# Second mixer of a two-block network: the two attention heads of a pair in common steps, kept cumulative sums, and scan products ordered by kind

## The reference

```python
# 8 heads of 64: strictly causal stick-breaking attention
z = q @ k.T * 64 ** -0.5
log_keep = where(valid, -softplus(z), 0)
log_rest = cumsum(log_keep, reverse=True) - log_keep
attn = where(valid, exp(log_sigmoid(z) + log_rest), 0);  o = attn @ v
# 8 heads of 64: RWKV-7 recurrence, one token after the other
sa = S @ (-kk_t)
S = S * w_t + outer(sa, kk_t * a_t) + outer(v_t, k_t);   y_t = S @ r_t
```

## Time and profile before

| | us |
|---|---|
| three runs: median (lowest, highest) | 2177.69 (2170.0, 2178.99) |
| the profiled execution, its time | 2169.75 |
| its span | 2168.5 |
| TensorE busy | 1991.5 (92%) |
| VectorE, ScalarE, GpSimd busy | 794.9, 705.6, 763.2 |
| chain that ended last: TensorE's share of the span | 28% (L489, the products with weights: 19%) |

### The profile page before, as it was taken

The page is one execution under the profiler, slowest core; times in us unless marked ns, Lnnn a source line. Parts: engine busy times, 40 slices in busy tenths (PEclk is TensorE's granted clock), DMA queues, the critical chain, the costliest instruction groups (busy, mean ns, idle before and its releaser), DMA issues. The chain is left out here.

```text
span 2168.5 us, 32158 instructions
## 1 busy us (share of the span) xinstructions
PE 1991.5 (92%) x13960; PEld 1674.6 (77%) x13960; DVE 794.9 (37%) x1065; ACT 705.6 (33%) x1056; POOL 763.2 (35%) x444
## 2 busy tenths in 40 slices
PE   3889988999999999999999888888999789999997
PEld 2657767777888889999999877866666568888885
DVE  6664453232111013443310466643443433434201
ACT  2453221333222333222222333254554333222222
POOL 2322120434444554444444332211111144444453
PEclk9999999999999999999999999998998899999999
DMA  7332220324332232232222422100000322332331
GB/s 272 115 119 98 79 79 32 116 78 145 117 97 90 90 102 88 88 94 91 84 88 93 131 59 63 30 6 2 2 2 2 126 69 89 96 97 89 98 91 62
DMA packets 55723, 182.76 MB, mean 84 GB/s; under 512 B 7552, under 2 KB 7808, under 8 KB 55456
## 3 DMA queue, kind: packets, MB, share of 16 engines
q1 hardware_dynamic: 55584, 180.72, 25.4%
HBM read 175.45 MB, written 5.24 MB: 83 GB/s over the span
## 5 line engine op out<-in xcount | busy, mean ns | idle before, releaser
L2090 POOL TENSOR_TENSOR WL<-RAWS,WH 128x1024 fp32r<-128x1024 f32 (+2 forms) x275 | 649.0, 2363 | 983.4 <-ACT WH L1622 983.4
L489 PE MATMUL PS<-HH,WH 128*128 128x264 f32 (+2 forms) x2184 | 673.1, 350 | 48.4 <-issue 12.9
L489 PE MATMUL PS<-HL,WH 128*128 128x264 f32 (+2 forms) x2184 | 657.4, 343 | 0.0
L489 PE MATMUL PS<-HH,WL 128*128 128x264 f32 (+2 forms) x2184 | 654.3, 341 | 0.0
L489 PEld LDWEIGHTS PS<-HH,WH 128*128 128x128 f32 (+1 forms) x2184 | 380.7, 192 | 117.4 <-issue 36.6
L1622 ACT ACTIVATE WH<-RAWS 128x1024 fp32r<-128x1024 f32 (+2 forms) x275 | 283.9, 1033 | 455.1 <-PE PS L489 402.1
L489 PEld LDWEIGHTS PS<-HH,WL 128*128 128x128 f32 (+1 forms) x2184 | 380.5, 191 | 48.4 <-issue 0.4
L489 PEld LDWEIGHTS PS<-HL,WH 128*128 128x128 f32 (+1 forms) x2184 | 380.9, 191 | 47.1 <-issue 1.6
L489 PE MATMUL PS<-IHf,WH 128*128 128x512 f32 (+1 forms) x704 | 209.4, 338 | 0.0
L489 PE MATMUL PS<-IHf,WL 128*128 128x512 f32 (+1 forms) x704 | 209.2, 338 | 0.0
L489 PE MATMUL PS<-ILf,WH 128*128 128x512 f32 (+1 forms) x704 | 209.2, 338 | 0.0
(11 more groups left out here) (493 smaller groups left out, 1917.0 us busy)
## 6 DMA issues: line engine op xcount, KB each, us to landing
RAWS<-w_w_in SPq DMA_DIRECT2D x52, 512.0 KB, 4.3
RAWS<-w_ada SPq DMA_DIRECT2D x32, 512.0 KB, 3.6
RAWS<-w_f0g SPq DMA_DIRECT2D x22, 512.0 KB, 3.6
RAWS<-w_f0u SPq DMA_DIRECT2D x22, 512.0 KB, 3.5
RAWS<-w_f1g SPq DMA_DIRECT2D x22, 512.0 KB, 3.6
RAWS<-w_f1u SPq DMA_DIRECT2D x22, 512.0 KB, 3.6
RAWS<-w_f2g SPq DMA_DIRECT2D x22, 512.0 KB, 3.5
RAWS<-w_f2u SPq DMA_DIRECT2D x22, 512.0 KB, 3.5
```

The costliest lines, as they stand in the source:

```text
L489: ins = te.matmul(ps[0:m, q, o:o + b - a] if len(halves) > 1 else ps[0:m, o:o + b - a], w[:, k * m:k * m + m], v[:, k0 + k, a:b], start=fi ...
L2090: ge.tensor_tensor(WL[s % NS][:, 0:n], RAW[i % NR][:, 0:n], WH[s % NS][:, 0:n].bitcast(f32), ALU.subtract).then_inc(*w_lo.up(s))
```

## The change

- `heads(b)` becomes `heads()`: both heads of a pair take each stage one after the other, in ten ticks a step instead of five. The round becomes five ticks of the recurrence and four of the heads. ATT_TICKS goes from 107 to 50.
- The sum of the masked values of all blocks done so far is kept: GpSimd adds the previous tile to the present one, ScalarE and VectorE split the sum into high and low parts at column 512 of KHI and KLO, and one pair of all-ones products takes the place of one per earlier block. Blocks' own parts all lie at column 0 (the first one at 512, where it is its own sum).
- The scan's value products read SV's lower half directly with 64 rows; V0, its zeros and its copy go, and `after_copy` with them.
- The scan's products with the state all come before those with the values, in both groups.
- `gn_g` and `gn_hi` become one semaphore each, in the same order.

```diff
-ATT_TICKS = 107
+ATT_TICKS = 50
@@ tensor, rw_scan
-            te.wait_ge(*rv0.at(n))
+            te.wait_ge(*ra[e].at("v", t))
...
             for i in range(4):
                 for par, q in enumerate(HALF):
-                    te.matmul(PS[q, 6, 64 * i:64 * i + 64], AR[:, i, n, 0, :], SB[:, i, par, :], start=True, stop=False)
-                    ins = te.matmul(PS[q, 6, 64 * i:64 * i + 64], MM[e][:, 2 * i + par, 0:64], V0[:, 2 * i + par, :],
-                                    start=False, stop=True)
+                    te.matmul(PS[q, 6, 64 * i:64 * i + 64], AR[:, i, n, 0, :], SB[:, i, par, :], start=i == 0, stop=False,
+                              skip_group_check=True)
+            for i in range(4):
+                for par, q in enumerate(HALF):
+                    ins = te.matmul(PS[q, 6, 64 * i:64 * i + 64], MM[e][64:128, 2 * i + par, 0:64],
+                                    SV[e][64:128, 2 * i + par, :], start=False, stop=True, skip_group_check=True)
...
                 for i in range(4):
                     te.matmul(PS[:, 6, 64 * i:64 * i + 64], SB[:, i, :, :].rearrange("p a t -> p (a t)"),
-                              AR[:, i, n, 1, :], start=True, stop=True)
-                    for par in range(2):
...
+                              AR[:, i, n, 1, :], start=i == 0, stop=False, skip_group_check=True)
+                for h in range(8):
+                    i, par = divmod(h, 2)
+                    ins = te.matmul(PS[64 * par:64 * par + 64, 6, 64 * i:64 * i + 64], SV[e][:, h, :],
+                                    MM[e][:, h, 64:128], start=False, stop=True, skip_group_check=True)
@@ tensor, heads
+                    for b, q in enumerate(HALF):
+                        te.matmul(PS[:, b, 0:n], KA[q, i, 128 * j:128 * j + 128], QA[q, i, 512 - n:512], start=True,
+                                  stop=True).then_inc(*hp[b].up("z", r))
+                    for _ in range(7):
+                        yield
+                    for b in range(2):
+                        te.wait_ge(*hd[b].at("lo", r))
                         for part in (KHI[b], KLO[b]):
+                            ins = te.matmul(PS[:, b, 0:n], TRIR[:, :], part[:, KAT[x]:KAT[x] + n], start=False, stop=True,
+                                            skip_group_check=True)
+                        if x:
+                            if x > 1:
+                                te.wait_ge(*hl.at(6 * i + 2 * x - 4 + b))
+                            m = LEN[j + 1]
+                            for part in (KHI[b], KLO[b]):
+                                ins = te.matmul(PS[:, b, n - m:n], ONER[:, :], part[:, 512:512 + m], start=False,
+                                                stop=True, skip_group_check=True)
+                        ins.then_inc(*hp[b].up("c", r))
+                    for _ in range(3):
+                        yield
...
                 for j in range(5):
+                    for b, q in enumerate(HALF):
+                        h = 2 * i + b
+                        ins = te.matmul(PS[q, b, 512 - LEN[j]:512], VT[:, j, 64 * h:64 * h + 64],
+                                        ATT[b][:, OFF[j]:OFF[j] + LEN[j]], start=(j == 0), stop=(j == 4))
@@ on every engine; vector and scalar with attention_parts() behind
-        alternate(rk, heads(0), rk, later_by(2, heads(1)))
+        rk, both = pipeline(NCH, rw_prepare, rw_scan), heads()
+        alternate(rk, both, rk, both, rk, both, rk, both, rk)
@@ vector: max-add at tick 4, then at tick 5 (x > 1) this, lower part at tick 6
+        def lower_sum(i, x, b):
+            n = LEN[BLOCKS[x]]
+            ve.wait_ge(*hh.at(6 * i + 2 * x - 2 + b))
+            ve.scalar_tensor_tensor(KLO[b][:, 512:512 + n], TT[b][(5 * i + x) % 2][:, 0:n], -1.0,
+                                    KHI[b][:, 512:512 + n].bitcast(f32), ALU.mult,
+                                    ALU.subtract).then_inc(*hl.up(6 * i + 2 * x - 2 + b))
@@ scalar: Abs, Exp, Ln of both heads at ticks 0, 1, 2, at 3 (x > 1) this, upper parts at 5, Exp into ATT at 8
+        def upper_sum(i, x):
+            r, n = 5 * i + x, LEN[BLOCKS[x]]
+            for b in range(2):
+                ae.wait_ge(*ht.at(6 * i + 2 * x - 2 + b))
+                ae.activation(KHI[b][:, 512:512 + n], TT[b][r % 2][:, 0:n], ACT.Copy,
+                              scale=-1.0).then_inc(*hh.up(6 * i + 2 * x - 2 + b))
@@ gpsimd: masks at ticks 4 and 9, between them at tick 7
+                    if x in (1, 2, 3):
+                        for b in range(2):
+                            t = TT[b][r % 2][:, 128:n]
+                            ge.wait_ge(*hd[b].at("lo", r))
+                            if x > 1:
+                                ge.wait_ge(*ht.at(6 * i + 2 * x - 4 + b))
+                            ge.tensor_tensor(t, t, TT[b][(r - 1) % 2][:, 0:n - 128],
+                                             ALU.add).then_inc(*ht.up(6 * i + 2 * x - 2 + b))
```

More of the change, by code:

```diff
@@ L933, in heads @@
                     r, n = 5 * i + x, LEN[j]
[L934 to L942, removed]
@@ L1529, in rw_scan, with heads @@
             yield
-        def heads(b):
+        def heads():
             for i in range(4):
@@ new lines, in heads @@
+                    for b in range(2):
+                        t = TT[b][r % 2]
+                        ve.wait_ge(*ha[b].at("ln", r))
+                        ve.scalar_tensor_tensor(t[:, 0:n], PS[:, b, 0:n], 0.0, t[:, 0:n], ALU.max,
+                                                ALU.add).then_inc(*hd[b].up("m", r))
+                        if j == 0:
+                            ve.wait_ge(*hd[b].at("m", r))
+                            ve.wait_ge(*fz.at("pm"))
+                            ve.tensor_scalar(t[:, 0:n], t[:, 0:n], PM[:, 0:1], None, ALU.mult).then_inc(*hm[b].up(i))
@@ L1561, in attention_parts @@
                                  ALU.subtract).then_inc(*cat2_lo.up(j))
-        ve.wait_ge(*rz.at("v0"))
-        ve.wait_ge(*rz.at("sb"))
+        ve.wait_ge(*rz.at(0))
         for s in s_bs:
             ve.wait_ge(s, 16)
-        rk = pipeline(NCH, rw_prepare, rw_scan)
-        alternate(rk, heads(0), rk, later_by(2, heads(1)), attention_parts())
+        rk, both = pipeline(NCH, rw_prepare, rw_scan), heads()
+        alternate(rk, both, rk, both, rk, both, rk, both, rk, attention_parts())
         def group_norm(i):
@@ L1992, in rw_scan, with heads @@
             yield
-        def heads(b):
-            pb, a = 64 * b, ha[b]
+        def heads():
             for i in range(4):
@@ L2007, in heads @@
-                    ae.activation(t, t, ACT.Ln, bias=1.0).then_inc(*a.up("ln", r))
+                    t = [TT[b][r % 2][:, 0:n] for b in range(2)]
+                    for b in range(2):
+                        ae.wait_ge(*hp[b].at("z", r))
+                        if x >= 2:
+                            ae.wait_ge(*ht.at(6 * i + 2 * x - 4 + b))
+                        ae.activation(t[b], PS[:, b, 0:n], ACT.Abs).then_inc(*ha[b].up("abs", r))
+                    yield
+                    for b in range(2):
+                        ae.wait_ge(*ha[b].at("abs", r))
+                        ae.activation(t[b], t[b], ACT.Exp, scale=-1.0).then_inc(*ha[b].up("exp", r))
```

151 lines of the change are left out of this document (66 added, 85 removed).

## The result

The change takes the kernel from 2176.26 us (median of 4 runs, 2170.0 to 2178.99) to 2155.66 us (4 runs, 2154.93 to 2156.39): a ratio of 0.991, with a 95% interval of 0.9893 to 0.9926. The direction was right, about a third of the size came.

What follows compares the result with a forecast made beforehand. It took the chain of a block, not TensorE's 220 us, as the new bound: four pairs of 60.6 us, 242, plus 3 make a 245 us mixer, 52 us less, so 2118, forecast 2120 us, range 2090 to 2155.

Steps and rivals of the forecast that it cites:

- What TensorE would save: Second mixer: 47 us less TensorE work, from 266.9 us busy to 220.
- The output pair: Two heads' products with the values, alternating column halves, overlap: about 3.2 us instead of 2 x 3.11, 12 us in all.
- The score pair: Two heads' score products on different row halves overlap: 1.5 us at 512 columns against 2 x 1.06, 10 us in all.
- The scan's output products: Ordered by kind in each of 8 scans: 1.3 us instead of 2.52, 9.8 us in all.
- Rival 3: The pairs of heads' products don't overlap on TensorE's array, 22 us come back: about 2135 us, chance 0.06.
- the loss of up to 12 us: By the Trainium skill's rule on weight loads, little of the output pair's 12 us would come.
- The static order: Five recurrent to four pair ticks a round: recurrence and attention end together, removing the last chunk's 40 us tail.
- The chain of a block: Dependent stages from scores to next scores as the mixer's new bound: 60.6 us a pair, 13.6 at x = 4.
- Rival 2: Queues in step bind each other, 1.5 us more in each of 20 blocks: mixer 275 us, time 2150, chance 0.17.
- Other engines: In the mixer ScalarE about 149 us busy, VectorE 140, GpSimd 51 of some 240; none becomes the bound.
- After the mixer: Output-weight and bonus loads and VectorE's wait for the bonus stay; cost 0, or 2.5 us without that cover.
- rival 4: TensorE's clock held low in the mixer: at a share of 0.6, 330 us and time 2203; chance 0.05.

Runs made afterwards that it cites:

- e5: Changed kernel with the output products of one head before those of the other instead of alternating: 2165.23 us, ratio 0.995 against the kernel before.
- e4: Changed kernel with only the scan's output products back in the old order, value products following each product with the state: 2167.58 us, ratio 0.9966 against the kernel before.
- e7: Changed kernel with four recurrent ticks instead of five to four of the heads in each round: 2171.05 us, ratio 0.9972 against the kernel before.
- e3: Kernel before with one more recurrent tick in each round, nothing else of the change: 2178.36 us, ratio 1.0021 against the kernel before.
- e1: Changed kernel made serial in the mixer, on every engine all recurrence first, then all paired heads: 2259.25 us, ratio 1.0384 against the kernel before.
- e13: Changed kernel with the recurrence one tick later in VectorE's queue only: 2149.39 us, ratio 0.9884 against the kernel before.
- e8: Changed kernel without the kept sums, each earlier block having its all-ones products again: 2151.59 us, ratio 0.99 against the kernel before.

## Why the prediction was wrong, point by point

1. *What TensorE would save: right.* 47 us forecast, 54 measured, as busy time. 64 all-ones products are left (eight rows of eight in the groups by shape), as said. The output pair, 20 products, holds TensorE from 1557.77 to 1560.93: 3.16 us, forecast 3.2, against 3.11 for one head in the earlier trace rows. The score pair at 512 columns holds it from 1537.97 to 1539.03: 1.06 us, forecast 1.5; it takes as long as one head did in the earlier trace rows. The scan's output products take 1.65 us (1539.65 to 1541.30), forecast 1.3, before 2.52: 7 us in eight scans, forecast 9.8. Rival 3 is out, and so is the loss of up to 12 us that the prediction set against the output pair; e5 (+9.6) and e4 (+12) show that these edits reached the time of the kernel.
2. *The static order as a gain of its own: too large.* The prediction calls it "the largest single effect". The tail did go: the last state update is at 1690.7 and the heads end 10 us later, twice the 5 us said. But the forecast let the 40 us vanish at the price of 0.64 us a recurrent tick. e7 shows what the removal gives in the paired form, 19 us of mixer for 44 us of tail. e3, meant to test it on the kernel before, made a new tail and settles nothing.
3. *The chain of a block: the step that failed.* The sum of 60.6 us a pair measured 68.4, mostly in x = 4, 13.6 forecast and 19.4 measured. The stages themselves were right: the second lower part is done 8.5 us after the scores' start in e1 (third pair), and the forecast's 9.1 to 9.7 less its 1.1 us of recurrent work is 8.0 to 8.6. What was wrong stands between the stages. Each recurrent operation there was priced at its length, 0.25 to 0.6 us. It should have been priced at the time when its own input arrives. Of the 14.9 us of the block above, 3.5 are such a wait before the first Exp, and more follow on VectorE and TensorE. The cumulative products were priced at full clock, which is 6.6 us of the whole. So x = 4 costs 23 us more over four pairs, and x = 2, whose waits were not taken apart, 8: together the 29 us between 245 and 274, the other blocks being about level and the forecast having 3 us in reserve.
4. *The recurrence as a chain: missing.* It was counted as TensorE work, 159 us, that fills gaps. e1 shows that it is 172 us long by itself, 145 of them busy. Two chains of 172 and, at a low clock, 207 us in fixed queues had to be laid into each other within 245; the forecast had no term for that.
5. *Rival 2 is what happened.* It gave 275 us of mixer and 2150 at a chance of 0.17; measured are 274 and 2155.7. Its price was spread evenly, 1.5 us in each of 20 blocks; in fact two of the five block lengths carry it, so that its sum came out is in part luck. The sign that it named (TensorE waits for recurrent copies) and the forecast's (for the lower part) both came, because each chain holds the other. e1 is the evidence for that: with the recurrence out of the way, scores to cumulative products at x = 4 fall from 13.6 to 8.2 us on average. e13 shows that the two waits trade: an edit that only changes which of the two comes first on VectorE takes 11 us from the one and gives 4 to the other.
6. *Other engines: sizes near, sign of the trade missed.* VectorE 132.5 of 140 forecast, ScalarE 133.3 of 149, GpSimd 53.3 of 51, the additions somewhat dearer than taken (0.51, 0.82 and 1.20 us on average for 128, 256 and 384 columns; 0.45, 0.78 and 1.1 taken). But in e8 the kept sums bring nothing that could be told from noise. Their 14 us on TensorE were the largest term of its 47, though the forecast itself had moved the bound to the chain, where their work on ScalarE and VectorE is a cost.
7. *After the mixer: right.* 453.1 us against 452.1; the first load is at 1701.06, and VectorE's wait for the bonus stayed.
8. *The clock: right in the mean, missed where it counts.* 0.90 in the mixer, 0.91 before, so rival 4 did not come. But in the changed kernel the low stretches lie in the long blocks (0.72 to 0.86), on the heads' chain, and the forecast had no term for that.

What stays open: how much of the 61 us of idle a better order would win, and how the excess in x = 4 divides between waits and clock beyond the 6.6 us. Only shifts of whole queues were tried, not an order made from the times at which inputs arrive.

## What to carry to other kernels

When two dependent chains share in-order queues, measure each alone (run them one after the other) before pricing their overlap: an operation of the other chain costs not its length but the wait for its own input, and that is set by the first chain. Removing a tail in which one chain runs alone gains only what the other chain has room for (here 19 of 44 us), and after such an edit look whether the other chain has got a tail instead. Work taken off an engine counts only while that engine is what the others wait for. Then shift one engine's queue by a tick against the rest: it is one word, and here it took up to 6 us off, a third of the whole change; on the wrong engine it cost 4.

## What the hardware did that I had not expected

**Two score products on different rows of the array cost as much as one here.** The earlier trace rows has 1.06 us for one head at 512 columns; the pair in the kernel after also holds TensorE 1.06. I had taken three lengths of four.

**VectorE's lower part is slower beside GpSimd.** At 1551.01 it takes 1.22 us and not 0.69 as at 1691.16, and the one after it, at 1552.15, takes 1.21. GpSimd starts its own tile products at 1550.85 and 1551.64 (L2177, 0.83 us, and L2178, 1.17 us); at 1691.16 it runs none, only a memset of 0.10 us. The Trainium skill, "SBUF — State Buffer", the section on the two separate sides, says that a VectorE operation with two inputs in SBUF and a GpSimd operation that reads SBUF share one pair of ports, held by one of them for a whole instruction; the trace agrees, with 0.53 us more twice in this block, and each time VectorE ends 0.55 us after GpSimd's product does. It cost the chain nothing here, since TensorE came to these products only at 1552.87 and 1554.74.

**The heads alone ran at a low clock, and it cost them time.** In the heads alone of e1, TensorE is nominally busy 97 of 207 us and its granted clock averages 0.59, so that most of the stretch has the lower of its two levels, 1.2 and 2.4 GHz. Its products lie on the chain there: those of 512 columns follow each other every 0.43 us (at 1740.86, 1741.29, 1741.71), in the changed kernel from 1555.58 on every 0.24. In the changed kernel's mixer the clock averages 0.90, but the long blocks have less, as said above. And e8, with 96 full-width products more in the mixer, has 0.95 where the changed kernel has 0.90, which may be why its extra work costs nothing; no run separates that from the shorter chain.
